# Regrouping the S5 inputs by 64 small SBUF transfers instead of two rounds of transposes, with three small products moved to column tiles

## What is computed

```python
def block(h, conv_st, ssd_st, s5r_st, s5i_st, mem_k, mem_v, p):
    proj = rmsnorm(h, p["norm_mix"]) @ p["w_in"]
    z, xbc, dt_raw, u = jnp.split(proj, ...)
    y_ssd, new_conv, new_ssd = ssd_mixer(z, xbc, dt_raw, conv_st, ssd_st, p)
    y_s5, new_re, new_im = s5_mixer(u, s5r_st, s5i_st, p)
    h = h + concatenate([y_ssd, y_s5]) @ p["w_out"]
    h = h + cross_attn(rmsnorm(h, p["norm_x"]), mem_k, mem_v, p["w_q"], p["w_o"])
    h = h + hmoe(rmsnorm(h, p["norm_ffn"]), p)
```

## Time and profile before

| | |
|---|---|
| median of 3 runs | 930.59 us (928.66 to 932.1) |
| profiled execution, its time | 932.57 us |
| its span in the trace | 930.8 us |
| TensorE busy | 864.2 us, 93% |
| TensorE weight loads (beside the products) | 682.8 us |
| VectorE, ScalarE, GpSimd busy | 350.1, 192.7, 136.2 us |
| mean granted TensorE clock | 0.968 of full speed |

### The profile page before, as it was taken

One profiled execution on the slowest core, in us unless ns is written; L12 is line 12 of the kernel. 1 busy time (PEld: TensorE's weight loads), 2 busy tenths in 40 slices (PEclk: granted clock), 3 DMA queues, 4 the chain that ended last, 5 costly groups with the idle time before them and its releaser, 6 DMA issues. The chain is left out here.

```text
span 930.8 us, 19000 instructions
## 1 busy us (share of the span) xinstructions
PE 864.2 (93%) x8017; PEld 682.8 (73%) x8017; DVE 350.1 (38%) x767; ACT 192.7 (21%) x432; POOL 136.2 (15%) x173
## 2 busy tenths in 40 slices
PE   3999999979999999999999998699999999999945
PEld 2778877867888888877889886576667767676722
DVE  5599896333642122410223456511111111111116
ACT  2312306434221110122221211111111111111103
POOL 1190100002420000000000000112222222222200
PEclk9999999989999999999999998599999999999977
DMA  9630072202121660071002033689999999999536
GB/s 245 212 98 1 5 183 91 91 12 93 47 91 68 226 237 1 1 226 46 1 5 104 29 114 154 251 305 350 336 370 359 369 377 364 386 377 372 228 83 245
DMA packets 71418, 166.48 MB, mean 179 GB/s; under 512 B 20592, under 2 KB 51440, under 8 KB 58496
## 3 DMA queue, kind: packets, MB, share of 16 engines
q1 hardware_dynamic: 58500, 150.86, 45.7%
q0 software_dynamic: 6144, 9.45, 3.1%
q10 hardware_dynamic: 6716, 5.34, 1.8%
HBM read 158.09 MB, written 17.88 MB: 189 GB/s over the span
## 5 line engine op out<-in xcount | busy, mean ns | idle before, releaser
L904 PE MATMUL bank<-act_a,weight_ring 128*128 128x288 f32 x768 | 192.9, 413 | 1.8 <-ACT act_a L1444 1.8
L904 PEld LDWEIGHTS bank<-act_a,weight_ring 128*128 128x128 f32 x768 | 147.8, 194 | 42.6 <-ACT act_a L1444 2.4
L1212 PE MATMUL bank<-weight_ring,act_b 128*128 128x256 f32 x512 | 111.9, 380 | 0.0
L1212 PEld LDWEIGHTS bank<-weight_ring,act_b 128*128 128x128 f32 x512 | 97.0, 190 | 12.7
L1381 PEld LDWEIGHTS bank<-region_t,weight_ring 128*64 128x64 f32 x2048 | 74.1, 142 | 14.3 <-issue 13.5
L1381 PE MATMUL bank<-region_t,weight_ring 128*64 128x80 f32 x2048 | 76.9, 237 | 1.9 <-issue 1.2
L1767 DVE TENSOR_TENSOR region_t<-region_t,bank 128x160 f32<-128x160 f32 (+3 forms) x47 | 15.5, 331 | 132.2 <-PE bank L1381 131.7
L830 POOL DMA_INDIRECT expert_rows<-region_r,scatter_now x32 | 30.1, 940 | 200.2 <-DVE region_r L2269 200.2
L1116 PE MATMUL bank<-weight_ring,region_u 128*128 128x256 f32 x256 | 58.3, 388 | 0.0
L2269 DVE COPY region_r<-bank 80x512 f32<-80x512 f32 x32 | 22.0, 687 | 96.3 <-PE bank L1393 96.3
L1393 PE MATMUL bank<-weight_ring,region_t 128*80 128x512 f32 x128 | 57.6, 593 | 0.0
(11 more groups left out here) (336 smaller groups left out, 1093.4 us busy)
## 6 DMA issues: line engine op xcount, KB each, us to landing
weight_ring<-in_w_gate SPq DMA_DIRECT2D x16, 1024.0 KB, 10.2
weight_ring<-in_w_down SPq DMA_DIRECT2D x16, 1024.0 KB, 12.5
weight_ring<-in_w_up SPq DMA_DIRECT2D x16, 1024.0 KB, 13.2
weight_ring<-in_w_in SPq DMA_DIRECT2D x8, 1024.0 KB, 8.4
region_g<-in_w_gate SPq DMA_DIRECT2D x8, 1024.0 KB, 11.1
region_g<-in_w_up SPq DMA_DIRECT2D x8, 1024.0 KB, 14.4
act_a<-in_w_down SPq DMA_DIRECT2D x8, 1024.0 KB, 13.3
act_a<-in_w_gate SPq DMA_DIRECT2D x8, 1024.0 KB, 11.4
```

What stands on the lines that cost most here:

```text
L904: m = pe.matmul(ps[:, 0:HALF], slot(c)[:, k, P * (mt % 2):P * (mt % 2 + 1)], x[:, k, HALF * h:HALF * (h + 1)], start=(k == 0), stop=(k == ...
L1212: m = pe.matmul(ps[0:L, CW * cc:CW * (cc + 1)], x[:, k, t0:t0 + L], slot(c)[:, k, :], start=(k == 0), stop=(k == KD - 1))
```

## The change

The two rounds of transposes are gone, with the ScalarE and VectorE copies between them. ScalarE's copy of u out of PSUM now writes uT sorted by token offset k, so that one channel's 72 values of an offset are one run of 288 bytes. Then 64 DMAs within SBUF (`regroup_u`), each for one k and one of eight groups within a 128-channel block, move 16 partitions x 4 blocks x 72 values to their place in U. SP issues those of k = 0 to 3, ScalarE those of k = 4 to 7; both wait for the last u copy. TensorE waits for all 64 before the first product of v.

The taps of 16 pairs go to four groups of 32 PSUM partitions in one bank (one job instead of four), with the four groups taking turns. The row sums of SSD go in halves of 64 tokens to partitions 0 to 63 and 64 to 127. In the sample steps of attention the two heads of a pair stand on partitions 0 to 63 and 64 to 127, so that the maximum, the exp, the division and the transposes take both at once. VectorE does the raw dt values in the midst of the scan, ahead of its fifth step, instead of behind it. The diff, cut to its core:

```diff
@@ plan_psum
-    for i in range(5):
-        if i < 4:
-            for h in range(2):
-                add("uj", "act", i, h)
-        if i >= 1:
-            for h in range(2):
-                add("ug", "dve", i - 1, h)
     for b in range(8):
         add("v", "dve", b)
-    for b in range(4):
-        add("tap", "act", b)
+    add("tap", "act")
@@ build
-        uT = mix[:, 4:8, :]
+        uT = mix[:, 4:8, :].rearrange("p i (k j) -> p i k j", k=Q8)
+        def regroup_u(eng, k):
+
+            for g in range(8):
+                eng.dma_start(U[GC * k:GC * (k + 1), g::8, :], uT[GC * g:GC * (g + 1), :, 7 - k, :]).then_inc(U_ready, 16)
@@ sync (SP)
             for c in range(2, CH_GLU):
                 load_chunk(c)
+            wait_emptied(sp, "u", 3, 1)
+            for k in range(Q8 // 2):
+                regroup_u(sp, k)
             sp.dma_start(w_rt[:, :, 0:NG], dram("w_router_group", "o (k p) n -> p (o k) n", p=P)).then_inc(route_loaded, 16)
@@ tensor
-            def u_blocks(i):
...
-            def u_turned(i):
...
-            u_blocks(0)
-            for i in range(4):
-                if i < 3:
-                    u_blocks(i + 1)
-                u_turned(i)
-
             for b in range(8):
                 ps = claim("v", b)
                 wait_emptied(pe, "wT", b)
-                wait_emptied(pe, "ug", b // 2, b % 2)
+                if b == 0:
+                    pe.wait_ge(U_ready, 16 * 8 * Q8)
...
-            for b in range(4):
-                ps = claim("tap", b)
-                if b == 0:
-                    pe.wait_ge(G_ready, 1)
-                    pe.wait_ge(bd_ready, 4)
-                for i in range(4):
-                    q = 4 * b + i
-                    for ri in range(2):
-                        m = pe.matmul(ps[0:32, P * i:P * (i + 1)], bd[:, ri, q, :], G[:, ri, q, 0:P],
+            ps = claim("tap")
+            pe.wait_ge(G_ready, 1)
+            pe.wait_ge(bd_ready, 4)
+            for i in range(4):
+                for ri in range(2):
+                    for part in range(4):
+                        q = 4 * part + i
+                        m = pe.matmul(ps[32 * part:32 * (part + 1), P * i:P * (i + 1)], bd[:, ri, q, :], G[:, ri, q, 0:P],
                                       start=(ri == 0), stop=(ri == 1))
-                m.then_inc(filled, 1)
+            m.then_inc(filled, 1)
...
                 for i in range(4):
-                    m = pe.matmul(ps[0:L, t:t + 1], sq[:, i, t0:t0 + L], ones[:, 0:1], start=(i == 0), stop=(i == 3))
+                    for half in range(L // HD):
+                        m = pe.matmul(ps[HD * half:HD * (half + 1), t:t + 1],
+                                      sq[:, i, t0 + HD * half:t0 + HD * (half + 1)], ones[:, 0:1],
+                                      start=(i == 0), stop=(i == 3))
...
+                    if L == NS:
                         for k in range(2):
-                            m = pe.matmul(ps[0:L, MEM * h:MEM * (h + 1)], mix[:, kk, t0:t0 + L], kT[seq][:, kk, :],
+                            for h in range(2):
+                                kk = 2 * (2 * hp + h) + k
+                                m = pe.matmul(ps[NS * h:NS * (h + 1), 0:MEM], mix[:, kk, t0:t0 + L], kT[seq][:, kk, :],
+                                              start=(k == 0), stop=(k == 1))
...
-                for h in range(2):
+                heads = 1 if L == NS else 2
+                for h in range(heads):
                     for k in range(2):
                         i = 2 * h + k
-                        m = turn(ps[:, P * i:P * i + L], PR[b][0:L, h, P * k:P * (k + 1)])
+                        m = turn(ps[:, P * i:P * (i + 1)], PR[b][:, h, P * k:P * (k + 1)])
...
+                            probs = PT[b][:, k, NS * h:NS * (h + 1)] if L == NS else PT[b][:, 2 * h + k, :]
@@ scalar
-                copy_out(uT[:, mt, HALF * h:HALF * (h + 1)], ps[:, 0:HALF])
+                copy_out(uT[:, mt, :, HALF // Q8 * h:HALF // Q8 * (h + 1)],
+                         ps[:, 0:HALF].rearrange("p (j k) -> p k j", k=Q8))
...
                 copy_u(mt, 1)
+            wait_emptied(act, "u", 3, 1)
+            for k in range(Q8 // 2, Q8):
+                regroup_u(act, k)
             act.wait_ge(G_ready, 1)
...
-            for b in range(4):
-                ps = wait_filled(act, "tap", b)
-                copy_out(tap[0:32, 4 * b:4 * b + 4, :].rearrange("p k c -> p (k c)"), ps[0:32, :])
+            ps = wait_filled(act, "tap")
+            for part in range(4):
+                m = act.activation(tap[0:32, 4 * part:4 * part + 4, :].rearrange("p k c -> p (k c)"),
+                                   ps[32 * part:32 * (part + 1), :], ACT.Copy)
+            m.then_inc(emptied["act"], 1)
@@ vector
-            for i in range(4):
-                for h in range(2):
-                    ps = wait_filled(dve, "ug", i, h)
-                    copy_out(U[:, 8 * i + 4 * h:8 * i + 4 * h + 4, :].rearrange("p g j -> p (g j)"), ps[:, 0:4 * NJ])
...
             for i in range(1, 8):
                 if i == 4:
                     add_skip()
+                if i == 5:
+                    raw_dt()
                 lam8_step(SSc[:, :, :, i], SSc[:, :, :, i - 1], SUP)
```

More of the change, by code:

```diff
@@ L760, in _ @@
             pool.memset(Tm, 0.0).then_inc(T_zero, 1)
-            wait_filled(pool, "tap", 3)
+            wait_filled(pool, "tap")
             pool.wait_ge(R_ready, 1)
@@ L1243, in scores @@
                         wait_emptied(pe, "q", 7, (n - NT) // 2)
-                    for h in range(2):
+                    if L == NS:
                         for k in range(2):
-                            kk = 2 * (2 * hp + h) + k
-                            m = pe.matmul(ps[0:L, MEM * h:MEM * (h + 1)], mix[:, kk, t0:t0 + L], kT[seq][:, kk, :],
-                                          start=(k == 0), stop=(k == 1))
+                            for h in range(2):
+                                kk = 2 * (2 * hp + h) + k
+                                m = pe.matmul(ps[NS * h:NS * (h + 1), 0:MEM], mix[:, kk, t0:t0 + L], kT[seq][:, kk, :],
+                                              start=(k == 0), stop=(k == 1))
+                    else:
+                        for h in range(2):
+                            for k in range(2):
+                                kk = 2 * (2 * hp + h) + k
+                                m = pe.matmul(ps[0:L, MEM * h:MEM * (h + 1)], mix[:, kk, t0:t0 + L], kT[seq][:, kk, :],
+                                              start=(k == 0), stop=(k == 1))
                     m.then_inc(filled, 1)
@@ L1952, in add_skip, with raw_dt @@
             def add_skip():
-                wait_emptied(dve, "tap", 3)
+                wait_emptied(dve, "tap")
                 tap0 = tap[0:32, :, 0:GC]
                 tt(tap0, tap0, dti[:, :].rearrange("p (q c) -> p q c", q=PAIRS), ALU.add).then_inc(tap_ready, 1)
+            d = dtt
+            def raw_dt():
+                ps = wait_filled(dve, "dt")
+                dve.wait_ge(small_loaded, 16 * SMALL_LOADS)
+                for par in range(2):
+                    half = slice(HD * par, HD * (par + 1))
+                    step(dve.tensor_copy(dsk[half, :], dsk_rows[half, par::2]))
+                link(dve.memset(d[:, 5, :], 0.0))
+                raw = d[:, 5, :].rearrange("p (t h) -> p t h", t=NT)
+                step(tt(raw[:, 0:4, :], ps[:, 0:32].rearrange("p (t h) -> p t h", t=4),
+                        dt_b[:, :].unsqueeze(1).to_broadcast([P, 4, HEADS]), ALU.add))
+                tt(raw[0:NS, 4, :], ps[0:NS, 32:40], dt_b[0:NS, :], ALU.add).then_inc(emptied["dve"], 1)
             for i in range(1, 8):
@@ L1991, in _ @@
             dve.tensor_copy(SS[:, :, 64], s5p[:, 3:5, :].rearrange("p r q -> p (r q)")).then_inc(h_ready, 1)
-            d = dtt
-            ps = wait_filled(dve, "dt")
-            dve.wait_ge(small_loaded, 16 * SMALL_LOADS)
-            for par in range(2):
-                half = slice(HD * par, HD * (par + 1))
-                step(dve.tensor_copy(dsk[half, :], dsk_rows[half, par::2]))
-            link(dve.memset(d[:, 5, :], 0.0))
-            raw = d[:, 5, :].rearrange("p (t h) -> p t h", t=NT)
-            step(tt(raw[:, 0:4, :], ps[:, 0:32].rearrange("p (t h) -> p t h", t=4),
-                    dt_b[:, :].unsqueeze(1).to_broadcast([P, 4, HEADS]), ALU.add))
-            tt(raw[0:NS, 4, :], ps[0:NS, 32:40], dt_b[0:NS, :], ALU.add).then_inc(emptied["dve"], 1)
-            sync()
             wait_emptied(dve, "dt")
```

45 lines of the change are left out of this document (15 added, 30 removed).

## The result

Four runs of the changed kernel gave a median of 916.8 us (914.83 to 917.46), beside 929.62 us (926.93 to 932.1) for the kernel before on the same chip: a ratio of 0.9865, 95% interval 0.9844 to 0.9885. The forecast was 917.6 in a range of 914.0 to 924.5. The profiled execution took 916.75 us, its span is 915.0 (before: 932.57 and 930.8).

The account below looks back on a forecast made before the run. TensorE was taken as the bound, busy 864.2 of 930.8 us. S5 9.4, row sums 1.1 and sample attention 2.5 sum to 13.0 us, taking the median of 930.59 to 917.6, range 914 to 924.5.

Parts of the forecast that it names:

- The regrouping leaves TensorE's row and is covered: S5 stage: 64 transposes and their waits leave TensorE, 6.1 us; transfers complete at 81, wanted at 93.6.
- Rival 1: Regrouping transfers of a queue wait for one another, U complete at 123.5: 947.5 us, slower; chance 0.05, milder form 0.05.
- Rival 3: Column tiles don't overlap at all: xBC only 5.9 us earlier, sums lose 3.3, 2.6 gained, 928; chance 0.03.
- rival 4: S5 gain given back later, at the load of w_out or the expert weights: 927; chance 0.05.
- Taps 2.0 us, xBC 10.9 earlier: S5 stage: taps in four alternating column groups take 2.0 against 7.07 us; xBC projection starts at 104.6, 10.9 earlier.
- A wait of 1.5 us at the ninth half, 9.4 left: xBC projection: TensorE waits 1.5 us for ScalarE's copy to free the first bank; 9.4 of 10.9 us are left.
- second slow stretch: xBC projection: the stall at the ninth half may cost another slow stretch of the clock, 1.8 us; none taken.
- Raw dt "keeps it there": xBC projection: moving raw dt into the scan keeps the wait at 1.5 us; dt's bank, wanted at 133.5, otherwise free at 135.
- Row sums 1.1: SSD row sums: 64 paired and 8 unpaired instructions take 3.1 us instead of 4.18, 1.1 us saved.
- Rival 2: SSD row sums lose 3.3 us by the split instead of saving 1.1: 922.0 us; chance 0.13.
- Attention 2.5: Sample attention, two steps of ten: paired scores and fewer transposes save 1.25 us each, 2.5 us; 0 from below.
- the S5 term: S5 stage: regrouping and taps start xBC 10.9 us earlier; less the wait of 1.5, 9.4 us gained.

Follow-up runs that it names:

- e7: The kernel before with the regrouping of u alone; taps, raw dt, row sums and sample attention as before: 922.49 us, ratio 0.993 to the kernel before.
- e4: The changed kernel with all 64 regrouping transfers issued by SP, none by ScalarE: 930.44 us, ratio 1.0004 to the kernel before.
- e0: The changed kernel run again, unedited: 918.53 us, ratio 0.9882 to the kernel before.
- e5: The changed kernel with the SSD row sums at full width again, as in the kernel before: 920.3 us, ratio 0.9917 to the kernel before.
- e6: The changed kernel with the sample tiles' attention as in the kernel before: 917.63 us, ratio 0.9882 to the kernel before.
- e2: The changed kernel with the taps as in the kernel before (four banks, one column group each): 917.68 us, ratio 0.9885 to the kernel before.
- e3: The changed kernel with the raw dt values behind the scan again, as in the kernel before: 918.94 us, ratio 0.9878 to the kernel before.
- e1: The changed kernel with ScalarE copying xBC tiles 0 and 1 ahead of its softplus work: 913.88 us, ratio 0.9833 to the kernel before.
- e8: e1 with VectorE's row statistics of tiles 5 and 6 moved ahead of the convolution's last tiles: 910.85 us, ratio 0.9815 to the kernel before.

## Why the prediction was right, and where not

- *The regrouping leaves TensorE's row and is covered.* Right, with v behind R's transposes without idle time; e7 has it alone at 6.9 us. The issue was mis-sized: 0.5 us was taken "nearer the small one", and it is 0.67 to 0.70, the dear end that the nearest form, the tap transfer, had shown. It cost nothing, since z copies were wanted only at 90.6 and had caught up at 85.9. With one queue it does matter, as e4 shows.
- *Rival 1, transfers one after another.* Refuted by e4. What did decide there was the issue. The landing, 2.0 us in the median, agrees with the 2.0 that the prediction took from the Trainium skill (DMA: Bandwidth & Descriptors, Anatomy of one DMA), though that section gives it for DMAs issued by GpSimd, and these came from SP and ScalarE. Rival 3 fell with the taps' 1.95 us, and rival 4 with the later stages: a row of router products just ahead of the expert stage starts 13.2 us earlier than before (561.50 against 574.70), and the end is 15.8 earlier.
- *Taps 2.0 us, xBC 10.9 earlier.* 1.95 and 10.67.
- *A wait of 1.5 us at the ninth half, 9.4 left.* The place and the releaser were right; it was 3.3 us. The step that failed: "TensorE gets there at 137.4" carried along the slow stretch behind the dtf wait, which in the changed kernel's first trace and in e0 didn't come, so TensorE arrived some 2 us earlier, 1.7 of it that stretch, and only waited longer. Where it did come, the forecast wait is there too. The trace of e5, whose program is the same up to the row sums, has the first eight halves in 33.0 us instead of 31.3, and then:

```profile
138.02 31.28 PE L904 MATMUL bank<-act_a,weight_ring 128*128 128x288 f32 x128 [1.65 <-ACT conv_io L1431]
```

  e6 has 1.63. The 9.4 itself doesn't depend on the stretch, since the bank sets it: e0's trace has 9.46. In the first trace the second slow stretch, which the prediction had considered and not taken, cost 2.8. By the same sum the taps were to bring 3.5 of the 9.4 (without them TensorE is 5.9 earlier and doesn't wait). In e2 y starts at 171.42 against 169.89, so 1.5, because the old taps, too, are spared the slow stretch; at the GLU 0.1 of it is left, and in the medians nothing.
- *Raw dt "keeps it there".* Correct as a mechanism: without it the bank of dt stops the eighth half. But the wait that it avoids is replaced by one as long a half later, so it is worth nothing by itself.
- *Row sums 1.1.* Mis-sized, 3.3 in the runs: the sums themselves won 1.7, since halves in pairs took 29 ns each and not 35, and the last group of 8 took 58 each and not 104; and the spared slow stretch, left to the range at up to 1.9, is worth 1.7 and was spared in all but one trace. Rival 2 was wrong.
- *Attention 2.5.* 2.1 on the timeline, 0 to 0.5 in the runs. The term was priced as 1.25 for each step, and step 9 won only 0.85: there the values product waits for ScalarE's copy 0.89 us instead of 0.72, so that the shorter transposes win nothing. By the medians it was 2.0 or more too high, about as much as the row sums' term was too low; how much of that is real the spread of the runs leaves open.

So 917.6 came out of 9.4 + 1.1 + 2.5 = 13.0. In its place the medians show about 6.9 for the regrouping (e7), 3.3 for the row sums, 0 to 0.5 for attention and nothing for taps or raw dt alone, in all 10.2 to 10.7, where the whole change has 10.5 in one group of runs and 12.8 in the other. The row sums' term was too low and the attention's probably too high. Whether the S5 term was too high is open: the regrouping alone gives 6.9, but in the six traces with the whole S5 edit or a part of it back on two queues (the first, e0, e2, e3, e5, e6) the row sums start 7.7 to 11.0 us earlier than in the one trace before, 9.5 in the mean. That the sum is nearer to what was measured than its terms is in part luck.

## What to carry to other kernels

Moving a transposition from TensorE to small transfers within SBUF pays when the data are ready long before they are wanted; count the issues, each at the price of the nearest form in the trace, and divide them among queues whose next work can wait. When an edit makes TensorE arrive earlier, ask which bank it meets then and where the engine that empties it stands in its own program: reordering that engine (e1, 1.6 to 4.6 us; e8, 3.6 more) can be worth as much as the edit, and decides whether further savings on TensorE, like the taps, show at all. Judge savings of 1 to 3 us by many runs and more than one trace, since some slow stretches of the clock come at other places in each; and look for one that is in all of them, since the wait ahead of it is worth more than its length (e8).

## What the runs showed of the hardware that was not expected

- Some of the granted clock's slow stretches come and go between executions of one program: behind the ninth half's wait the clock is 0.50 to 0.76 in the first trace (138 to 146) and 1.00 in e0. Over the fourteen traces, the wait of 1.5 us ahead of xBC has one behind it in seven, and the wait of 1.1 us ahead of the GLU in five (17.45 instead of 15.76 us). The wait of 4.2 us within y has one in all thirteen traces that have that wait. Some stand behind busy stretches like the full-width row sums. During a long idle time the clock falls and stays down: in e4, where TensorE waited from 93.9 to 103.9, the windows read

```profile
96.00:98.00 2.00, 0.00 (x0) 0.00 (x0) 0.00 (x0) 0.00 (x0) 0.00 (x0) 0.64 0.16 28
98.00:104.00 6.00, 0.09 (x2) 0.12 (x4) 0.00 (x0) 0.00 (x0) 0.00 (x0) 0.50 0.17 28
```

  and v ran in 5.58 us instead of 4.22.
- A float32 instruction with a single moving column took 112 ns with 128 columns of weights, 58 ns with 64, and 29 ns as one of a series of 64-column ones that takes turns on two column halves.
- The 64 transfers of 16 partitions took 0.60 to 0.62 us of a sequencer each, with 64 pieces of 288 bytes, where the tap transfers with 256 pieces took 0.61: the issue didn't depend on the number of pieces.
